# A mixture-of-experts step: the first main tile from four token tiles, an early gather, and one ring of weight buffers

## The reference

```python
g_logit = (t @ w_grp + b_grp)
_, g_idx = lax.top_k(g_logit, 1)                 # one of 4 groups
e_sel = take_along_axis(e_logit, g_idx)          # 4 experts of the group
top_v, top_i = lax.top_k(e_sel, 2)               # two of them
w_top = softmax(top_v) * g_p
for e in range(16):
    he = silu(t @ w1[e]) * (t @ w3[e])           # 1024 -> 512
    y = y + combine[:, e:e + 1] * (he @ w2[e])   # 512 -> 1024
x = x + gate2 * y
```

## Time and profile before

| | us |
|---|---|
| median of 3 runs | 1193.85 (1192.95 to 1195.25) |
| the profiled execution | 1192.73 |
| its span, first to last instruction | 1190.9 |
| PE busy in the span | 1141.0 (96%) |
| first expert product starts | 899.63 |
| last expert product starts | 1172.21 |

### The profile page before, as it was taken

How to read it: one execution, slowest core, us unless ns; L and a number is a source line. 1 busy time by engine, 2 the same in 40 slices (tenths; PEclk the granted TensorE clock), 3 DMA queues, 4 the chain that set the end, 5 groups by cost and what they waited for, 6 DMA issues and landing times.

```text
span 1190.9 us, 14573 instructions
## 1 busy us (share of the span) xinstructions
PE 1141.0 (96%) x5774; PEld 707.4 (59%) x5775; DVE 535.2 (45%) x1046; ACT 226.3 (19%) x478; POOL 353.5 (30%) x289
## 2 busy tenths in 40 slices
PE   3999999999999999999999999999969999999995
PEld 2666777777777777777777777755544333333342
DVE  3664477454785683383334334535573121211121
ACT  4222366223570002001100010002111111111010
POOL 1585400467003343333333333000001123223222
PEclk9999999999999999999999999999979999999998
DMA  9955020022200222222222215531169999999982
GB/s 351 341 208 202 24 80 3 17 71 80 80 1 1 71 71 72 71 71 71 71 71 71 71 70 208 199 141 71 71 247 382 409 408 411 402 407 402 403 314 29
DMA packets 54005, 200.86 MB, mean 169 GB/s; under 512 B 5616, under 2 KB 6192, under 8 KB 47792
## 3 DMA queue, kind: packets, MB, share of 16 engines
q1 hardware_dynamic: 47056, 185.20, 40.3%
q0 software_dynamic: 6272, 13.13, 4.2%
q10 hardware_dynamic: 608, 1.58, 0.3%
HBM read 189.36 MB, written 18.91 MB: 175 GB/s over the span
## 4 chain that ended last, share of the span: by engine, by line
PE 90%; DMA 7%; DVE 2%; issue 0%; ACT 0%; POOLq 0%; SPq 0%; POOL 0%; DVEq 0%
PE psum L2291 35%; PE psum L2078 12%; PE psum L2468 6%; PE psum L2355 6%; PE psum L2199 4%; PE psum L2055 4%; DMA arena<-in_w 3%; PE psum L2259 3%; PE psum L2492 3%; PE psum L2470 2%; PE psum L2544 2%; PE psum L2530 2%; DMA weight_ring<-in_w 2%; PE psum L2003 2%; PE psum L2233 1%; DMA weight_ring<-in_w_ada 1%
## 5 line engine op out<-in xcount | busy, mean ns | idle before, releaser
L2291 PE MATMUL psum<-arena,weight_ring 128*128 128x320 f32 x928 | 256.9, 432 | 0.0
L2291 PEld LDWEIGHTS psum<-arena,weight_ring 128*128 128x128 f32 x928 | 175.9, 190 | 72.7
L779 POOL TENSOR_TENSOR weight_ring<-weight_ring 128x512 f32<-128x512 f32 x80 | 107.9, 1349 | 348.6 <-DMA weight_ring<-in_w_in 196.1
L2291 PE MATMUL psum<-x,weight_ring 128*128 128x320 f32 x640 | 179.5, 432 | 0.0
L2291 PEld LDWEIGHTS psum<-x,weight_ring 128*128 128x128 f32 x640 | 121.1, 190 | 49.6
L780 POOL TENSOR_TENSOR weight_ring<-weight_ring 128x512 f32<-128x512 f32 x80 | 111.7, 1397 | 0.0
L1563 DVE TENSOR_TENSOR arena<-psum,arena 128x320 f32<-128x320 f32 x124 | 59.5, 488 | 93.2 <-PE psum L2291 92.4
L2078 PE MATMUL psum<-weight_ring,x 128*128 128x256 f32 x384 | 88.0, 380 | 0.0
L2468 PE MATMUL psum<-weight_ring,arena 128*32 128x512 f32 x512 | 77.2, 593 | 2.8 <-DMA arena<-in_w 1.7
L2078 PEld LDWEIGHTS psum<-weight_ring,x 128*128 128x128 f32 x384 | 71.7, 190 | 11.3 <-issue 1.1
L2355 PE MATMUL psum<-weight_ring,arena 128*128 128x512 f32 x160 | 71.8, 596 | 0.0
(11 more groups left out here) (345 smaller groups left out, 1520.7 us busy)
## 6 DMA issues: line engine op xcount, KB each, us to landing
arena<-in_w SPq DMA_DIRECT2D x22, 2048.0 KB, 19.0
weight_ring<-in_w SPq DMA_DIRECT2D x21, 2048.0 KB, 24.2
weight_ring<-in_w_in SPq DMA_DIRECT2D x15, 2048.0 KB, 8.5
arena<-in_w_ada SPq DMA_DIRECT2D x6, 2048.0 KB, 13.2
x<-in_w SPq DMA_DIRECT2D x5, 2048.0 KB
x<-in_x_sample SPq DMA_DIRECT2D x2, 2048.0 KB, 12.4
arena<-in_w_ada SPq DMA_DIRECT2D x4, 1024.0 KB, 14.6
weight_ring<-in_w_ada SPq DMA_DIRECT2D x4, 1024.0 KB, 14.4
```

What stands on the lines that cost most here:

```text
L779: nc.gpsimd.tensor_tensor(out[:, 0:2], a_[:, 0:2], b_[:, 0:2], op)
L2291: last = mm(product_psum(q, name), w[:, k, :], src[:, k, :], start=(k == 0), stop=(k == 3))
```

## The change

Couple 0 is laid out differently. Its main tile has 64 rows of a and 64 of b, which may come only from the first four token tiles. The rows of a and b that are left, up to 32 each, go into the first half of half tile 0, beside couple 1's 64. `first_places` and `first_hots` make a table of one column from ranks that are known before the context tile is routed; `first_table` sums it on PE in the midst of `choose(4)`, and POOL gathers the first tile from the latent rows at once. Only gate a and gate b of couple 0 are loaded beside it; up a waits for the gather. The tables of the other tiles stand between the last five steps of the first gate product. The late product's steps move ahead of it, filler products (`keep_busy`, into a free bank) stand in gaps, and the late transpose moves behind the first half tile's gate and up product. `half_gate_up(0)` and `half_down(0)` multiply with both experts of couple 0. Half tile 0 is added in three pieces. All nine buffers form one ring (`HOME`, `HELD_BY`): a load takes the buffer that PE is to free next. The second half of `gate1`'s product goes from POOL to DVE.

The core of the diff:

```diff
+def freed_in_order():
+    freed = [(part, which, 0) for part in ("gate", "up") for which in "ab"]
+    for t in range(1, COUPLES - 1):
+        freed += [("gate", "a", t), ("up", "a", t), ("gate", "b", t), ("up", "b", t), ("down", "a", t)]
+        if t == 1:
+            freed.append(("down", "a", 0))
+        if t % 2:
+            freed += [("down", "b", t - 1), ("down", "b", t)]
+    return freed
+HOMES = 9
+LOADS = [name for t in range(COUPLES) for name in matrices(t)]
+HELD_BY = dict(zip(LOADS[HOMES:], freed_in_order()))
...
+def main_lanes(t):
+    return ((0, 64, "a"), (64, P, "b")) if t == 0 else ((0, 32, "a"), (32, 64, "a"), (64, 96, "a"), (96, P, "b"))
+def half_lanes(j):
+    first = ((0, 32, "a", 0), (32, LANE, "b", 0)) if j == 0 else ((0, LANE, "b", 2 * j),)
+    return first + ((LANE, P, "b", 2 * j + 1),)
...
             sp.wait_ge(s_order, 1)
+            load("gate", "a", 0, a)
+            job_done(sp, "wo", 2 * NT - 1)
+            load("gate", "b", 0, b)
+            sp.wait_ge(s_xg[0], 16)
+            load("up", "a", 0, a)
+            sp.wait_ge(s_outx, 16 * CTX)
+            load("up", "b", 0, b)
...
             pool.wait_ge(s_slot, 1)
-            pool.wait_ge(s_h2out, 16 * NT)
+            pool.wait_ge(s_h2out, 16 * CTX)
+            gather(0, idxc[:, 0:1], s_xg[0], N_LAT)
+            pool.wait_ge(s_slot, 2)
+            pool.wait_ge(s_last_h2out, 16)
...
+            def first_places():
+                second, far, apart, start = part16[0], part16[2], part16[4], part16[5]
+                link(V.tensor_scalar(apart, far, 1.0, float(EMPTY), ALU.is_ge, mult))
+                link(V.scalar_tensor_tensor(out=start, in0=second, scalar=float(EARLY_ROWS), in1=apart, op0=mult, op1=add))
...
             residual(2 * NT - 1)
+            dve.wait_ge(s_x2, 2 * NT)
+            V.tensor_tensor(gate1[:, 0, 512:D], x_sb[:, D * CTX + 512:D * NT], mod2[:, 0, 1, 512:D], mult).then_inc(s_last_wide, 1)
             rank_distance()
             x2_sum(NT - 1)
-            place_rules()
+            first_places()
             x2_rstd(NT - 1)
             dve.sem_inc(s_last_rstd, 1)
-            choose(NT - 1)
+            first_hots()
+            choose(NT - 1, first_slots)
             dve.wait_ge(s_last_scaled, 1)
             h2_shifted(NT - 1)
+            place_rules()
...
+            def first_table():
+                for n in range(2 * CTX):
+                    if n % CTX == 0:
+                        pe.wait_ge(s_hot, n // CTX + 1)
+                    last = mm(first_psum, first_hot[:, n, :], pair_vals[:, n // 2:n // 2 + 1], start=(n == 0), stop=(n == 2 * CTX - 1))
+                last.then_inc(s_table, 1)
...
+            ada_part(LAST_PAIR, late_psum, range(1, 2), late_slot)
+            first_table()
+            ada_part(LAST_PAIR, late_psum, range(2, 3), late_slot)
+            keep_busy(1, 1)
             rank(NT - 1)
             count(NT)
...
+            next_tokens(0)
+            pe.wait_ge(s_xgT, TOKEN_TILES.index(0) + 1)
+            main_part(0, "gate", gate_psum, range(0, KT - NT))
+            for i in range(NT):
+                last = main_part(0, "gate", gate_psum, range(KT - NT + i, KT - NT + i + 1))
+                if i == NT - 1:
+                    last.then_inc(s_gate_mm, 1)
+                table(i)
```

More of the change, by code:

```diff
@@ L266 @@
[L266 to L276, removed]
@@ L279, in down_count, with matrices @@
-def down_count(which, t):
-    name = (which, t)
-    return sum(DOWN_UNIT[n] == DOWN_UNIT[name] for n in DOWN_LOADS[:DOWN_LOADS.index(name) + 1])
+def matrices(t):
+    if t + 1 == COUPLES:
+        return [(part, which, t) for part, which in (("gate", "b"), ("up", "b"), ("gate", "a"), ("down", "b"), ("up", "a"), ("down", "a"))]
+    return [(part, which, t) for part in ("gate", "up", "down") for which in "ab"]
+def freed_in_order():
[7 more added lines that the diff above has]
+    return freed
@@ new lines, in _ @@
+            sp.wait_ge(s_late, 1)
+            load("gate", "a", 1, a)
+            load("gate", "b", 1, b)
+            sp.wait_ge(s_wtable, NT)
+            load("up", "a", 1, a)
+            load("up", "b", 1, b)
+            load("down", "a", 1, a)
+            load("down", "b", 1, b)
+            for t in range(2, COUPLES):
+                a, b = expert_at(COUPLES - 1 - t), expert_at(COUPLES + t)
+                for part, which, _ in matrices(t):
+                    load(part, which, t, a if which == "a" else b)
@@ L1688, in tile_upto, with choose @@
                 return rt[i][:, 48:64]
-            def choose(i):
+            def choose(i, between=None):
                 v = int(i == CTX)
@@ L2489, in half_gate_up @@
                 lo, up, gate = half_base(t), half_base(t), LANE - half_base(t)
+                if t == 0:
+                    gate_a, up_a = weights("gate", "a", t), weights("up", "a", t)
+                    for k in range(KT):
+                        for row, gate_k, up_k in ((0, gate_a[:, k, :], up_a[:, k, :]), (32, gate_w[:, k, :], up_w[:, k, :])):
+                            tokens = xgT_half[:, k, row:row + 32]
+                            mm(half_psum[LANE + row:LANE + row + 32, :], tokens, gate_k, start=(k == 0), stop=(k == KT - 1))
+                            last = mm(half_psum[row:row + 32, :], tokens, up_k, start=(k == 0), stop=(k == KT - 1))
+                    last.then_inc(s_half_mm, 1)
+                    return
                 for k in range(KT):
@@ L2537, in half_down @@
                 pe.wait_ge(s_hhT_half, 2 * j + 2)
-                first, second = down_weights("b", 2 * j), down_weights("b", 2 * j + 1)
+                lanes = [(lo, hi, weights("down", which, t)) for lo, hi, which, t in half_lanes(j)]
                 for half in range(2):
```

313 lines of the change are left out of this document (156 added, 157 removed).

## The result

The changed kernel took 1198.94 us in the median of 5 runs (1197.86 to 1199.24), beside 1194.43 for the kernel before in the same rounds (1192.95 to 1195.56, 5 runs). The ratio is 1.0039, with a 95% interval of 1.0028 to 1.005: slower by 0.4%. I had forecast 1191.0, in a range that ended at 1196.5. The profiled execution took 1197.86 us, its span is 1196.1.

A forecast was written before the change was run, and what follows sets the result against it. PE was taken to set the time from the first expert product, weight stream hard behind. Of 2.0 + 3.3 = 5.3 us gained, POOL's chain left 1.2 + 1.6 = 2.8 off: 1191.0 us, range 1187.5 to 1196.5.

The forecast's parts named there:

- one more piece at 8.5 less 0.5: POOL's adds of half tile 0: third piece costs 8.0 us more, bounds 5 and 9.5.
- the sum's 1031.4: Gather behind half tile 0: landed at 1018.0 before, forecast 13.4 us later through POOL's late chain.
- First gate product at 889.4: Start of PE's expert stage: early gather lands at 887, gate product starts 10.2 us earlier than before.
- my bounds: Landing of the first tile's early gather: taken as 887, with ends 884.5 and 892.7.
- rival C: PE at half clock around the first gate product, starting it about 893.5: 1197.0 us or 1198; chance 0.14.
- Late transpose 12.0 later, main_down(0) 2.0 earlier: PE's order after the first gate product: late transpose at 921.0, first down product at 923.4.
- The three matrix waits go: PE's waits on expert matrices, 1.7, 1.0 and 0.6 us, vanish: 3.3 us off, ends 0 and 3.3.
- The chain of adds: POOL's gathers and output adds, in one order: 13.4 us late by the gather behind half tile 0.
- rival B: POOL's chain has room: added piece 5 us or less, or gather lands in 10; 1188.5 us; chance 0.23.
- the wait of 2.5: PE at the second half tile's tokens waits 2.5 us on the gather, leaving 1.2 us of gain there.
- The fast part alone, 5.3 us: Gain without POOL's price: 2.0 us from earlier main_down(0) plus 3.3 from matrix waits.

The follow-up runs named there:

- e1: Changed kernel with half tile 0's down product in four column groups of 32 instead of 32, 32 and 64: 1196.12 us, ratio 1.0019.
- e2: Kernel before, with only half tile 0's down product put in column groups of 32, 32 and 64 instead of 64 and 64: 1199.4 us, one run.
- e5: e1 with the late transpose and table write moved ahead of the weight tables and second token transpose: 1188.72 us, ratio 0.9956.
- e3: Changed kernel with half tile 0's down product sorted by width, the two groups of 32 first, then the 64: 1197.04 us, one run.
- e6: e1 with half tile 0 added in two pieces of 64 rows instead of three of 32, 32 and 64: 1191.68 us, one run.
- e10: Changed kernel with only the earlier late transpose and table write, down product still in 32, 32 and 64: 1197.89 us, ratio 1.0027.

## Why the prediction was wrong

**The step that failed** is one that the prediction doesn't contain. It priced everything about half tile 0's three groups on POOL ("one more piece at 8.5 less 0.5") and took PE's down product over at the old 7.0 us. The product took 15.95. This is 8.9 us, against a forecast that missed by 7.9.

With the product alone put right the forecast would still have been too low: e1, where it takes 7.07 us, measured 1196.12. There the gather landed at 1036.1, 4.7 us later than the sum's 1031.4 (1018.0 and 13.4), and the half clock behind PE's wait cost 2.5. That makes 7.2 us, beside 6.7 by which e1's span (1194.8) is above the forecast's (1190.9 less 2.8).

The other steps, in their order:

- **First gate product at 889.4:** 890.79, and 1.1 of the 1.4 is already there ahead of the routing of the last tile (DVE's steps of it at 870.64 against 869.51). Right. The early gather was issued at 880.21 and landed by 888.5, inside my bounds. The fillers ended at 888.5, not near 886, since they ran at half clock up to about 886 (0.53 in 882 to 886). From there on the clock was at 1.00, so rival C did not come, though 878 to 892 averages 0.76.
- **Late transpose 12.0 later, main_down(0) 2.0 earlier:** 13.4 later (922.34 against 908.98), and level (925.38 against 925.40). For both, 1.4 is the later start; for the second, 0.8 is a wait on DVE's one-hots that I hadn't in the sum.
- **The three matrix waits go:** they went, but e2 shows them gone in the old buffers as soon as PE loses 8.9 us. In e5, where PE isn't held up, they stay away at the places of the earlier trace rows. What the ring itself is worth was not tried: the old two sets of buffers can't hold the new layout, because down matrices of couples 0 and 1 are all alive until half tile 0.
- **The chain of adds:** the late write, three pieces of 8.9, 9.5 and 9.5 us, a gather issued 3.3 us ahead of the forecast. The mechanism was right and hidden in the changed kernel. Two sizes were off and partly cancelled. The added piece cost 3.5 us up to the gather (992.94 to 1014.88, against 986.28 to 1004.76) and not 8.0, which meets rival B's condition of 5 us or less; and the chain came to half tile 0 6.7 us late and not 5.4. With the groups mended (e1) they are 4.6 and 12.1, and the gather is 3.3 us behind the forecast: a wait of 4.6 where I had 2.5. The term left out was what a wait does afterwards: 2.5 us of half clock.
- **The fast part alone, 5.3 us (rival B's 1188.5):** e5 takes the chain's price away and measures 5.2 off (1188.72 against 1193.91 beside it). That the totals agree is partly luck. The 3.3 of the matrix waits is there; the 2.0 of the earlier `main_down(0)` is not: in e5 that product starts at 927.14, 1.7 later than before (925.40), as much as half clock cost at `main_up(0)`; without it it would be level, as in the changed kernel. From there to the last expert product e5 wins 3.9 us, 0.6 more than the waits. And the two profiled executions are only 2.6 us apart (1190.16 and 1192.73): e5's is 1.4 slower than its median, before's 1.2 faster than the median beside it.

From the first gate product to the end of the span I had 298.7 us (1190.9 less 2.8 less 889.4) and the changed kernel took 305.3. Of the 6.6 more, 8.9 are the product, the wait of 2.5 that I had put in is absent, and the way from the gate product to `main_down(0)` took 0.6 more (34.6 against 34.0). This balances to 0.4.

## What to carry to other kernels

- When a tile is cut anew, price the product on PE as well as the moves around it. In these runs column groups ran side by side only when all had one width: cut a group of 64 into two of 32 rather than let it stand beside narrower ones.
- A stage that shows fewer waits can be slower: compare the duration of the same product in both traces before looking at waits.
- Two faults on parallel chains must be mended together. Each repair alone looked nearly worthless (2.8 and 1.1 us), both were worth 10.2.

## What the runs showed of the hardware

- Groups of unlike width (32 and 64) don't overlap: 15.95 us for 32, 32 and 64, against 7.07 for four of 32. Each change of width costs 0.13 us beyond that (15 changes against 3 in e3's 14.34).
- Beside the weight stream an accumulating piece took longer with more rows and behind a gather: behind a gather 13.0 us for 64 rows (e6) and 11.2 for 32 (e1), behind another piece 9.3 (e6) and 8.0 (e1).
- A wait of PE of 4.6 us in the midst of full work brought the clock to 0.50 and cost 2.5 us more. A wait of 3.1 and 3.3 us at the first gather, in e6 and e10, also ended in half clock.
- The same fall came in e1 and e5 without any wait, for some 3 us at the start of `main_up(0)`, behind products of 4 and 12 columns, and not there in the changed kernel or its other variants. In e3 it came later: 0.50 from 916 to 918 us, at the start of half tile 0's gate and up product, behind products of 1 to 5 columns, short transposes and 1.2 us of idle time. It costs 1.7 to 1.8 us where it comes; what sets it off stayed open. In e5 (PE busy, granted clock, DMA share, GB/s):

```profile
900.00:902.00 2.00, 2.00 (x14) 1.00 0.94 401
902.00:904.00 2.00, 2.00 (x15) 0.79 1.05 451
904.00:906.00 2.00, 2.00 (x8) 0.50 1.04 442
906.00:908.00 2.00, 2.00 (x10) 0.86 1.00 428
```
